# 32 bytes of padding behind each row of two TensorE operand buffers

## The chip, the cores and the metric

The kernel runs on one core of one Trainium2 chip. A core has five engines with their own instruction streams: TensorE (PE in the profile, with its weight loads as PEld), VectorE (DVE), ScalarE (ACT), GpSimd (POOL) and SyncE (SP), which issues most DMA transfers. SBUF is the working memory of 128 partitions; PSUM, in eight banks, takes TensorE's results. The metric is the device time of one execution in microseconds (us), as the median of several runs; lower is better.

## What is computed

Two transformer-like blocks over 256 tokens of width 2048, all in 32-bit floats. Cut to what matters here, the work is a chain of matrix products with 256 tokens on one side:

```
proj = rmsnorm(x) @ w_in                      # 2048 -> 7168, first block
x = x + mix @ w_out                           # attention and a gated recurrence in mix
x = x + softmax(q k) v @ w_mo                 # attention over 256 memory rows
x = x + (silu(a) * b) @ w_down                # a, b = conv(rmsnorm(x) @ w_up); 5632 wide
# second block: w_in_2, three conv mixers, w_out_2, then
f = (silu(gate) * val) @ w_down_2             # gate, val = conv(rmsnorm(x) @ w_up_2)
x = x + rms_norm(f)
```

## The kernel before

Each 32-bit matrix is split into a high part (rounded to the format fp32r, which TensorE multiplies in one pass) and a low part (the rest). A product A·B is then three products: hi·hi, lo·hi and hi·lo. The weights come in chunks of 128 partitions x 1024 floats: SP's queue loads a chunk to one of four slots of `raw`, ACT rounds it to `w_hi` (L784), DVE subtracts to make `w_lo` (L1325), and TensorE uses both. The semaphores `raw_loaded`, `hi_rounded`, `chunk_split` and `chunk_used` tie the four together, four chunks deep. Nothing of this is touched by the change.

The activations stand in two buffers with the same layout. `op` (the operand) has KT = 16 rows to a partition, one for each 128 features; `gu` (the gated buffer, named g in the profile) has FT = 44 rows. A row is 256 floats of the high part and behind them 256 floats of the low part, so it has 2048 bytes. `op_hi`, `op_lo`, `g_hi` and `g_lo` are views of them. `op` starts at byte 91456 of a partition and `gu` at the start of the arena, byte 124224; both are 320 past a multiple of 512 and so is each of their rows. `raw`, `w_hi` and `w_lo` start at 16512, 32896 and 49280, each 128 past such a multiple; a tile of 128 weights is 512 bytes, so each tile begins there too.

TensorE runs the products in three shapes, all through the helper `mm` (L2107):

- **The HHLL shape** (`product_halves` for up, down and up_2, and the parts of kind Q in `one_part`): the weight tile is stationary. Two matmuls of w_hi with the whole row (hi and lo, 512 columns), then two of w_lo with the row's first half (256 columns). A group is four matmuls, 1536 columns.
- **The three-times-256 shape** (parts of kind F, and conf, pool and gated in `product`): w_hi·hi, w_hi·lo, w_lo·hi for one weight tile, each with 256 columns; three matmuls, 768 columns.
- **The token-major shape** (hg_i, da_v, mem_v, out_2, down_2): 128 tokens of a row are stationary and 512 weights move past; three matmuls, 1536 columns. out_2 reads `y_hi` and `y_lo`, which the change doesn't pad.

```
mm(ps[:, 4 * parity + t], w_hi[:, s, cs], both[:, k].rearrange("p a t -> p (a t)"), k == 0, False)
mm(ps[:, 4 * parity + t, TOK:2 * TOK], w_lo[:, s, cs], both[:, k, 0], False, k == g.kt - 1)
```

In a line of the profile such as `ps<-op,w_hi`, the result is ps and the two operands follow; where the weights are stationary the activation stands first (`op,w_hi`), in the token-major shape it stands last (`w_hi,op`).

ACT writes the high parts (`round_pair`, `head_hi` and others), two or four rows with one instruction at most; DVE writes the low parts (`low_pair` L1398, `rest_of` L1390, `low` in `feed_forward`). Behind `gu` in the arena stand `up_s`, `cg` and `cv`, which hold the products of up while the convolution is made. The scratch for sums of squares, `sumsq` among it, is placed from the arena's end, at arena + 96928 + 4096 = byte 225248.

Of the kernel before, what the change touches and what calls it, by code (L numbers as in the profile page):

```python
# [19 lines left out]
F32R = mybir.dt.float32r  # L20
# [5 lines left out]
P = 128  # L26
TOK = 256
DM = 2048
KT = DM // P
FF = 5632  # L30
FT = FF // P
# [5 lines left out]
CONF_TAPS = 31  # L37
WB = 768
SLOTS = 4
CW = 1024  # L40
BANK = 512
EPS = 1e-6
# [6 lines left out]
UPAD = 2  # L49
# [38 lines left out]
def pieces_of(name, b):  # L88

    return [Piece(part.kind, part.bank + i, part.chunk + part.chunks) for part in parts_of(name, b) for i in range(part.tiles // 2)]  # L90
# [133 lines left out]
def build(nc, A):  # L224
# [4 lines left out]
    with ctx:  # L229
        at = [16512]  # L230

        def place(name, shape, dt=F32, offset=None):
            size = 4
            for d in shape[1:]:
                size *= d
            where = at[0] if offset is None else offset
            if offset is None:
                at[0] += (size + 31) // 32 * 32
            return nc.alloc_sbuf_tensor_at(name, shape, dt, offset=where)

        def sem(name):
            return ctx.enter_context(nc.semaphore(name))


        raw = place("raw", [P, SLOTS, CW])
        w_hi = place("w_hi", [P, SLOTS, CW], F32R)
        w_lo = place("w_lo", [P, SLOTS, CW], F32R)
        x_at = at[0]
# [10 lines left out]
        rstd = place("rstd", [P, 2, TOK])  # L259
        ones_r = place("ones_r", [P, P], F32R)  # L260
        op_at = at[0]
        op = place("op", [P, KT, 2, TOK], F32R)
        op_hi, op_lo = op[:, :, 0], op[:, :, 1]
        arena = at[0]
        end = 229344
        room = end - arena
        KB = 1024

        def inside(name, shape, offset, dt=F32):
            size = 4  # L270
            for d in shape[1:]:
                size *= d
            assert offset + size <= room, (name, offset, size, room)
            return place(name, shape, dt, offset=arena + offset)


        st = (room - 8 * KB) // 32 * 32
        sqb = inside("sqb", [P, 2, 2, TOK], st)
        sumsq = inside("sumsq", [P, 2, TOK], st + 4 * KB)
        sumsq_w = inside("sumsq_w", [P, 2, TOK], st + 6 * KB)  # L280
        sq_all = inside("sq_all", [P, 8, 2, TOK], 62 * KB)
        sq_in = inside("sq_in", [P, 8, 2, TOK], 0)
        hbuf = inside("hbuf", [P, 4, 2, TOK], 84 * KB)


        slab = lambda name, kb: inside(name, [P, HEADS, TOK], kb * KB)
        da_q, da_k = slab("da_q", 0), slab("da_k", 24)
        v_da, v_hg = inside("v_da", [P, 2, CW], 56 * KB), inside("v_hg", [P, 2, CW], 56 * KB)
        bias = slab("bias", 80)
# [28 lines left out]
        mp = inside("mp", [P, 2, TOK], 56 * KB)  # L318
        mp_t = inside("mp_t", [P, 2, 2, TOK], 58 * KB)

        gu = inside("g", [P, FT, 2, TOK], 0, F32R)
        g_hi, g_lo = gu[:, :, 0], gu[:, :, 1]
        up = inside("up_s", [P, 4, UPAD + TOK], 2 * FT * KB)
        cg = inside("cg", [P, 4, TOK], 2 * FT * KB + 16 * (UPAD + TOK))
        cv = inside("cv", [P, 4, TOK], 2 * FT * KB + 16 * (UPAD + TOK) + 4 * KB)

        y_hi = inside("y_hi", [P, KT, TOK], 0, F32R)
        y_lo = inside("y_lo", [P, KT, TOK], 16 * KB, F32R)
# [27 lines left out]

        raw_loaded = [sem(f"raw_loaded{i}") for i in range(SLOTS)]
        params_loaded, consts_loaded, norm_loaded = sem("params_loaded"), sem("consts_loaded"), sem("norm_loaded")
# [72 lines left out]
        def own_pieces(g, b, k):  # L431

            early = lambda p: p.kind == "F" and p.chunks < g.chunks
            return [i for i, p in enumerate(pieces_of(g.name, b)) if p.chunks + SLOTS - early(p) == k and p.chunks < g.chunks]

        def late_pieces(g, b, k, slots):

            if (g.name, b) in PARTS:
                return [i for i, p in enumerate(pieces_of(g.name, b)) if k == SLOTS and p.chunks == g.chunks]
            return [k - SLOTS] if slots is None else slots.get(k, ())  # L440
# [151 lines left out]
        def _(sp):  # L592
# [12 lines left out]
            sp.dma_start(raw[:, 0, 0:BANK], A["weights"][first_source, :, 0:BANK]).then_inc(first_loaded, 16)  # L605
            sp.dma_start(raw[:, 0, BANK:CW], A["weights"][first_source, :, BANK:CW]).then_inc(raw_loaded[0], 16)
            for c in range(1, KT):
# [167 lines left out]
        def _(act):  # L775
            steps = Steps(act, act_steps)

            def split(u, s):

                act.wait_ge(raw_loaded[s], 16 * u + 16)  # L780
                if not isinstance(u, int) or u > 0:

                    act.wait_ge(chunk_used, SLOTS * u + (s - SLOTS + 1))
                nc.scalar.activation(w_hi[:, s], raw[:, s], ACT.Copy).then_inc(hi_rounded, 1)  # L784
# [88 lines left out]
            act.wait_ge(raw_loaded[0], 16)  # L873
            nc.scalar.activation(w_hi[:, 0, BANK:CW], raw[:, 0, BANK:CW], ACT.Copy).then_inc(hi_rounded, 1)
            split(0, 1)
# [1920 lines left out]
```

## Time and profile before

| what | us |
|---|---|
| median of 3 runs | 2634.1 |
| lowest and highest | 2633.75 and 2635.73 |
| the profiled execution, its own time | 2635.15 |
| its span, first to last instruction | 2633.4 |
| PE busy in it | 2621.2 |
| PEld (weight loads, beside PE) | 2316.8 |
| DVE busy | 1789.2 |
| ACT busy | 1345.3 |
| POOL busy | 150.8 |
| mean granted TensorE clock | 0.999 of 2.4 GHz |

A matmul's duration in the profile runs past the start of the next one, since they are pipelined. What a matmul costs in a stream is the distance from its start to the start of the next, and the timeline gives the starts; its rows merge neighbours of the same kind, with their number behind x.

### The profile page before, as it was taken

Reading aid. Unit: us, or ns where it says so; the run is one execution under the profiler, and the core shown is the slowest. Engines: PE = TensorE matmul, PEld = TensorE weight load, DVE = VectorE, ACT = ScalarE, POOL = GpSimd, SP = SyncE. Lnnn points to the kernel's source line nnn. Section 1 sums busy time; section 2 is a strip of 40 time slices with the busy share of each in tenths; the row PEclk is TensorE's granted clock in tenths of the full one; section 3 lists DMA queues with packets and bytes.
Section 4 is the critical chain, followed back from the end, with each engine's and each line's share of the span. In section 5 each row is a group of like instructions: output and inputs, shape, how many; then the busy total and the mean of one; then the engine's idle time right before and its main releaser. Section 6 shows DMA issues by size and latency. Waiting matters only on the chain.

```text
span 2633.4 us, 41690 instructions
## 1 busy us (share of the span) xinstructions
PE 2621.2 (100%) x15689; PEld 2316.8 (88%) x15689; DVE 1789.2 (68%) x2188; ACT 1345.3 (51%) x1647; POOL 150.8 (6%) x106
## 2 busy tenths in 40 slices
PE   9999999999999999999999999999999999999999
PEld 9888898889999888888888889998888888888887
DVE  7677567566645777777775456998777777776444
ACT  6554375464533655555553344444665555554443
POOL 2001200000200200000001222000020000000000
PEclk9999999999999999999999999999999999999999
DMA  8555455546535555555555555655565555556554
GB/s 264 193 160 186 140 184 186 176 156 203 184 130 169 188 193 188 189 190 188 188 191 191 189 189 180 200 198 166 173 193 190 189 188 189 191 191 207 192 191 146
DMA packets 256256, 487.12 MB, mean 185 GB/s; under 512 B 15069, under 2 KB 80629, under 8 KB 255616
## 3 DMA queue, kind: packets, MB, share of 16 engines
q1 hardware_dynamic: 254496, 476.11, 54.7%
q0 software_dynamic: 1488, 9.19, 1.0%
q8 instruction: 92, 1.51, 0.2%
q14 instruction: 36, 0.29, 0.0%
q10 hardware_dynamic: 144, 0.01, 0.0%
HBM read 483.12 MB, written 2.13 MB: 184 GB/s over the span
## 4 chain that ended last, share of the span: by engine, by line
PE 92%; DVE 5%; ACT 1%; POOL 1%; issue 1%; DMA 0%; SPq 0%; DVEq 0%; ACTq 0%; POOLq 0%
PE ps L2107 92%; DVE w_lo L1325 2%; DVE acc L1854 2%; POOL sumsq L724 1%; DMA raw<-in_weights 0%; ACT w_hi L784 0%; DVE ua L1359 0%; DVE ya L1918 0%; DVE x_res L2088 0%; ACT lnz L1219 0%; PE ps L2640 0%; PE ps L2427 0%; DVE y_lo L1390 0%; DVE ya L1920 0%; DVE pa L1883 0%
## 5 line engine op out<-in xcount | busy, mean ns | idle before, releaser
L1325 DVE TENSOR_TENSOR w_lo<-raw,w_hi 128x1024 fp32r<-128x1024 f32 x899 | 1117.6, 1246 | 767.4 <-ACT w_hi L784 766.1
L2107 PE MATMUL ps<-op,w_hi 128*128 128x512 f32 (+1 forms) x6208 | 1615.0, 350 | 0.7 <-DVE op L1398 0.6
L784 ACT ACTIVATE w_hi<-raw 128x1024 fp32r<-128x1024 f32 x899 | 949.0, 1059 | 1083.3 <-PE ps L2107 1051.0
L2107 PEld LDWEIGHTS ps<-op,w_lo 128*128 128x128 f32 x5024 | 944.5, 188 | 163.8
L2107 PE MATMUL ps<-op,w_lo 128*128 128x256 f32 x5024 | 1086.7, 278 | 0.0
L2107 PEld LDWEIGHTS ps<-op,w_hi 128*128 128x128 f32 x6208 | 939.0, 188 | 5.2 <-issue 2.8
L2107 PE MATMUL ps<-g,w_hi 128*128 128x512 f32 x704 | 219.6, 393 | 0.0
L2107 PE MATMUL ps<-w_hi,g 128*128 128x512 f32 x704 | 218.3, 391 | 0.0
L2107 PE MATMUL ps<-w_hi,op 128*128 128x512 f32 x512 | 164.5, 396 | 0.0
L2107 PEld LDWEIGHTS ps<-g,w_lo 128*128 128x128 f32 x704 | 132.4, 188 | 30.0
L2107 PEld LDWEIGHTS ps<-w_hi,g 128*128 128x128 f32 x704 | 132.3, 188 | 27.9
L2107 PE MATMUL ps<-g,w_lo 128*128 128x256 f32 x704 | 138.8, 278 | 0.0
L2107 PE MATMUL ps<-w_lo,g 128*128 128x512 f32 x352 | 138.0, 392 | 0.0
L2107 PEld LDWEIGHTS ps<-w_hi,op 128*128 128x128 f32 x512 | 96.2, 188 | 22.2 <-issue 1.3
L2107 PEld LDWEIGHTS ps<-g,w_hi 128*128 128x128 f32 x704 | 106.0, 188 | 0.0
L2107 PE MATMUL ps<-w_lo,op 128*128 128x512 f32 x256 | 100.1, 391 | 0.0
L2107 PEld LDWEIGHTS ps<-w_lo,g 128*128 128x128 f32 x352 | 66.1, 188 | 15.4
L1854 DVE SCALAR_TENSOR_TENSOR acc<-glu,par,acc 128x256 f32<-128x256 f32 x180 | 74.9, 474 | 0.0
L1751 DVE SCALAR_TENSOR_TENSOR cg<-up_s,par,cg 128x256 f32<-128x256 f32 x176 | 73.3, 478 | 0.0
L1751 DVE SCALAR_TENSOR_TENSOR cv<-up_s,par,cv 128x256 f32<-128x256 f32 x176 | 73.3, 478 | 0.0
L2107 PEld LDWEIGHTS ps<-w_lo,op 128*128 128x128 f32 x256 | 48.1, 188 | 9.8
L1740 DVE TENSOR_TENSOR up_s<-up_s,rstd 128x1024 f32<-128x1024 f32 x44 | 53.9, 1225 | 1.5
(318 smaller groups left out, 1535.0 us busy)
## 6 DMA issues: line engine op xcount, KB each, us to landing
raw<-in_weights SPq DMA_DIRECT2D x899, 512.0 KB, 4.3
x_res<-in_x SPq DMA_DIRECT2D x8, 256.0 KB, 6.1
mem_x<-in_mem POOLq DMA_DIRECT2D x1, 2048.0 KB, 8.4
x_res<-in_x POOLq DMA_DIRECT2D x1, 2048.0 KB, 9.7
w_row<-row_dram POOLq DMA_DIRECT2D x2, 1024.0 KB, 7.4
out_x<-x_res SPq DMA_DIRECT2D x3, 512.0 KB, 2.9
rel_rev<-rel_dram POOLq DMA_DIRECT2D x1, 1024.0 KB, 7.7
hg_con<-in_hg_consts POOLq DMA_DIRECT2D x1, 576.0 KB, 5.3
```

What stands on the lines that cost most here:

```text
L724: steps.inc(TT(sumsq[:, :, :], squares[:, 0] if j == 1 else sumsq[:, :, :], squares[:, j], ALU.add))
L784: nc.scalar.activation(w_hi[:, s], raw[:, s], ACT.Copy).then_inc(hi_rounded, 1)
L1325: TT(w_lo[:, s], raw[:, s], w_hi[:, s].bitcast(F32), ALU.subtract).then_inc(chunk_split, 1)
L1740: TT(up[:, :, UPAD:UPAD + TOK], up[:, :, UPAD:UPAD + TOK], spread(rstd[:, 1], 4), ALU.mult).then_inc(up_scaled, 1)
L1751: ins = STT(buf[:, t], up[:, t, tap:tap + TOK], col(tap, kind, t, b), buf[:, t], ALU.mult, ALU.add)
L1854: ins = STT(acc[:, i], glu[:, i, tap:tap + TOK], pc("conv_b_w_2", 6 * tap + i), acc[:, i], ALU.mult, ALU.add)
L2107: return nc.tensor.matmul(out, lhsT, rhs, start=start, stop=stop, skip_group_check=True)
```

## The change

A constant ROW_PAD = 8 floats (32 bytes) is added behind each row of `op` and `gu`. The row pitch goes from 2048 to 2080 bytes. The sixteen rows of `op` then begin at sixteen different places within 512 bytes, 320 + 32·k modulo 512, and the 44 rows of `gu` go through these places 2.75 times. The views leave the padding out, so each row is still read and written as 512 neighbouring floats. `op` is 512 bytes longer, so the arena begins 512 bytes later; `gu` is 44·32 = 1408 bytes longer, and `up_s`, `cg` and `cv` move behind it. Everything counted from the arena's end stays at its byte. On every engine the instructions, their order and their semaphore waits are the same before and after.

```
@@ -37,6 +37,7 @@
 SLOTS = 4
+ROW_PAD = 8
 CW = 1024
@@ -259,12 +260,13 @@
         op_at = at[0]
-        op = place("op", [P, KT, 2, TOK], F32R)
+        op = place("op", [P, KT, 2 * TOK + ROW_PAD], F32R)[:, :, 0:2 * TOK].rearrange("p k (a t) -> p k a t", a=2)
         op_hi, op_lo = op[:, :, 0], op[:, :, 1]
         arena = at[0]
         end = 229344
         room = end - arena
         KB = 1024
+        GATED_END = FT * (2 * KB + 4 * ROW_PAD)
@@ -318,11 +320,11 @@
-        gu = inside("g", [P, FT, 2, TOK], 0, F32R)
+        gu = inside("g", [P, FT, 2 * TOK + ROW_PAD], 0, F32R)[:, :, 0:2 * TOK].rearrange("p k (a t) -> p k a t", a=2)
         g_hi, g_lo = gu[:, :, 0], gu[:, :, 1]
-        up = inside("up_s", [P, 4, UPAD + TOK], 2 * FT * KB)
-        cg = inside("cg", [P, 4, TOK], 2 * FT * KB + 16 * (UPAD + TOK))
-        cv = inside("cv", [P, 4, TOK], 2 * FT * KB + 16 * (UPAD + TOK) + 4 * KB)
+        up = inside("up_s", [P, 4, UPAD + TOK], GATED_END)
+        cg = inside("cg", [P, 4, TOK], GATED_END + 16 * (UPAD + TOK))
+        cv = inside("cv", [P, 4, TOK], GATED_END + 16 * (UPAD + TOK) + 4 * KB)
```

## Rows read from the trace of the kernel before

**Rows 1.** The page: busy time, share of the span and instructions; the chain by engine.

```profile
PE 2621.2 (100%) x15689; PEld 2316.8 (88%) x15689; DVE 1789.2 (68%) x2188; ACT 1345.3 (51%) x1647; POOL 150.8 (6%) x106
...
PE 92%; DVE 5%; ACT 1%; POOL 1%; issue 1%; DMA 0%; SPq 0%; DVEq 0%; ACTq 0%; POOLq 0%
```

**Rows 2.** Waits of TensorE, the longest: total us, times, longest.

```profile
PE ps L2107 <- DVE w_lo L1325: 1.7, 2, 1.5
```

**Rows 3.** TensorE's instructions by shape: count, busy us, mean ns, idle before.

```profile
L2107 PE MATMUL ps<-op,w_hi 128*128 128x512 f32 x3840 | 1201.1, 394 | 0.1
L2107 PE MATMUL ps<-op,w_lo 128*128 128x256 f32 x5024 | 1086.7, 278 | 0.0
L2107 PE MATMUL ps<-op,w_hi 128*128 128x256 f32 x2368 | 414.1, 280 | 0.6 <-DVE op L1398 0.6
L2107 PE MATMUL ps<-g,w_hi 128*128 128x512 f32 x704 | 219.6, 393 | 0.0
L2107 PE MATMUL ps<-w_hi,g 128*128 128x512 f32 x704 | 218.3, 391 | 0.0
L2107 PE MATMUL ps<-w_hi,op 128*128 128x512 f32 x512 | 164.5, 396 | 0.0
...
L2107 PE MATMUL ps<-w_hi,y_hi 128*128 128x512 f32 x128 | 51.3, 401 | 1.7 <-DVE w_lo L1325 1.7
```

**Rows 4.** Timeline of TensorE, three-times-256, at 670 us: start, length.

```profile
669.79 0.39 PE L2107 MATMUL ps<-op,w_hi 128*128 128x256 f32 x2
...
670.81 0.39 PE L2107 MATMUL ps<-op,w_hi 128*128 128x256 f32 x2
```

**Rows 5.** The same shape at 1750 us, in gated.

```profile
1749.73 0.40 PE L2107 MATMUL ps<-op,w_hi 128*128 128x256 f32 x2
...
1750.79 0.40 PE L2107 MATMUL ps<-op,w_hi 128*128 128x256 f32 x2
```

**Rows 6.** Timeline of TensorE, HHLL from op, in up at 1000 us.

```profile
999.71 0.62 PE L2107 MATMUL ps<-op,w_hi 128*128 128x512 f32 x2
1000.17 0.40 PE L2107 MATMUL ps<-op,w_lo 128*128 128x256 f32 x2
...
1001.79 0.62 PE L2107 MATMUL ps<-op,w_hi 128*128 128x512 f32 x2
```

**Rows 7.** TensorE in a stretch of down, HHLL from g: busy (matmuls), clock, DMA.

```profile
1400.00:1550.00 150.00, 150.00 (x867) 1.00 0.57 189
```

**Rows 8.** Timeline of TensorE, token-major from g, in down_2.

```profile
2500.06 0.62 PE L2107 MATMUL ps<-w_hi,g 128*128 128x512 f32 x2
...
2502.12 0.39 PE L2107 MATMUL ps<-w_hi,g 128*128 128x512 f32 x1
```

**Rows 9.** Timeline of TensorE, token-major from y, in out_2.

```profile
1795.02 0.40 PE L2107 MATMUL ps<-w_hi,y_lo 128*128 128x512 f32 x1
...
1796.42 0.40 PE L2107 MATMUL ps<-w_hi,y_lo 128*128 128x512 f32 x1
```

**Rows 10.** Timeline of TensorE, head means, ones_r stationary, eight matmuls of 512.

```profile
337.96 0.40 PE L2107 MATMUL ps<-hg_sq_high,ones_r 128*128 128x512 f32 x1
...
338.43 0.39 PE L2107 MATMUL ps<-hg_sq_high,ones_r 128*128 128x512 f32 x1
...
339.12 0.39 PE L2107 MATMUL ps<-hg_sq_low,ones_r 128*128 128x512 f32 x1
...
339.57 0.39 PE L2107 MATMUL ps<-hg_sq_low,ones_r 128*128 128x512 f32 x1
```

**Rows 11.** A stretch of up, PE, PEld, DVE, ACT, POOL busy (instructions), clock, DMA.

```profile
1000.00:1200.00 200.00, 200.00 (x1156) 175.44 (x1155) 145.76 (x171) 109.83 (x127) 0.00 (x0) 1.00 0.57 189
```

**Rows 12.** Matmuls that read sumsq, and that read lnz: ns min/median/max.

```profile
L2107 PE MATMUL ps<-sumsq,con x16: 378/379/454, 50.5 to 1925.8; 128*128 128x256 f32 x16
...
L2107 PE MATMUL ps<-lnz,con x12: 377/379/379, 1829.3 to 1831.7; 128*128 128x256 f32 x12
```

**Rows 13.** Timeline in up: DVE's split of one chunk and its idle time before.

```profile
1299.89 1.22 DVE L1325 TENSOR_TENSOR w_lo<-raw,w_hi 128x1024 fp32r<-128x1024 f32 x1 [0.85 <-ACT w_hi L784]
```

## The prediction

> **What bounds the kernel now.** I read the page first. Its busy line gives TensorE 2621.2 us of a span of 2633.4, and the chain that ended last is 92% TensorE [rows 1]. The view of waits then asks whether TensorE starves: its longest entry is 1.7 us in all [rows 2]. So the time is the sum of the distances between matmul starts, and the other engines matter only where they would make TensorE wait. The groups by shape give the counts, the timeline gives the distances, and I read one for each shape.
>
> - HHLL from `op`: groups start at 999.71 and, three later, at 1001.79, so 2.08/3 = 0.693 us for 1536 columns [rows 6]. From `gu` it is the same: 867 matmuls in 150 us, 4 × 150/867 = 0.692 [rows 7]. In up, 1156 matmuls in 200 us give 0.692 as well [rows 11].
> - Three-times-256: nine matmuls from 669.79 to 670.81 are 0.1133 us each [rows 4]; at 1750 us, same code and same places in SBUF modulo 512, nine take 1.06 us, 0.1178 each [rows 5]. About half of this shape runs at each pace.
> - Token-major from `gu`: nine matmuls from 2500.06 to 2502.12, 0.229 each, 0.687 for three [rows 8]. From `y`: six in 1.40 us, 0.233 each, 0.700 for three [rows 9].
>
> At 2.4 GHz (the stretches show a granted clock of 1.00 [rows 7, 11]) 1536 columns are 0.640 us, so each shape loses 6 to 10% of its time to something between the columns. If the change acts, it acts there.
>
> **The change, part by part.** It removes and adds no instruction; every engine keeps its order and waits. Four things move.
>
> *Places of the rows that TensorE reads.* Counts [rows 3]: 3840/2 + 704/2 = 1920 + 352 = 2272 HHLL groups; 2368/2 = 1184 groups of three times 256, 3552 matmuls; token-major 704/2 = 352 groups from `gu`, 512/2 = 256 from `op` (and 128 from `y`, whose row pitch stays). At today's paces these are 2272 × 0.692 = 1572 us, 3552 × 0.1156 (the mean of the two) = 411, 352 × 0.687 + 256 × 0.687 = 418, and 128 × 0.700 = 90: 2491 of the 2633.4. What would another place do? No operand row stands anywhere else modulo 512 than 320, so the trace can't price it directly; it can show how much the distances differ by themselves, and whether they follow place.
>
> They don't follow it much where I can look. (a) Two paces, 0.1133 and 0.1178, with the same places, in long unbroken stretches [rows 4, 5]: the pace is kept from whatever state the stream was in when it last restarted. (b) In nearly all products the activation row and the weight tile that is loaded meanwhile begin 192 bytes apart modulo 512 (320 against 128). In the head means both `ones_r` and the squares begin at 320, zero apart. There two matmuls take 0.47 us at first (337.96 to 338.43) and two take 0.45 near the end (339.12 to 339.57), 1.61/7 = 0.230 on the mean [rows 10]; the band with another distance is that of the token-major stretches, 0.229 and 0.233 [rows 8, 9]. (c) DVE busy for 145.76 of 200 us, ACT for 109.83 and DMA at 0.57 don't disturb the paces [rows 11]: HHLL is 0.69 per group wherever I look, so it isn't a meeting with other engines that the padding would space out. I take 0 for this edit.
>
> *Bounds of it, from both sides.* The fastest that the rows show is 0.225 for 512 columns (0.45/2 [rows 10]) and 0.1133 for 256 [rows 4]; the slowest 0.235 (0.47/2 [rows 10]) and 0.1178 [rows 5]. If each shape ran at its fastest: HHLL 2 × 0.225 + 2 × 0.1133 = 0.677, less 0.015 × 2272 = 34 us; three-times-256 less 0.0023 × 3552 = 8; token-major 0.675, less 0.012 × 608 = 7. Together −49 us. At the slowest: HHLL 2 × 0.235 + 2 × 0.1178 = 0.706, plus 0.014 × 2272 = 32; three-times-256 plus 0.0022 × 3552 = 8; token-major 3 × 0.235 = 0.705, plus 0.018 × 608 = 11. Together +51 us.
>
> By the Trainium skill (TensorE: Matmul & The Clock Gate, Back-to-back issue gap) an isolated matmul costs N/2.4 + 2.5 ns, some 216 ns for 512 columns and 109 for 256. The rows here show 0.225 to 0.235 and 0.113 to 0.118, so the trace is slower than that rule in each shape; if the places were the whole of the difference and the change took it away, an estimate by that page would be 2 × 0.216 + 2 × 0.109 = 0.650 for HHLL, which is 0.042 × 2272 = 95 us less in that shape alone.
>
> *Places of the rows that ACT and DVE write.* A pair of rows or four rows now step by 520 floats and not by 512. These writes are off the path: in up DVE has 0.85 us of idle time before the 1.22 us split of a chunk [rows 13], and TensorE's waits on it sum to 1.7 us in the whole kernel [rows 2]. Any slowing up to that idle time is hidden; if the cover were gone, w_lo would be late next and TensorE would wait at `chunk_split`. Cost 0; on both sides I allow a microsecond.
>
> *`up_s`, `cg`, `cv` and the arena.* They are read and written by DVE and ACT alone, under the same cover. The arena moves by 512 bytes, so nothing else in it changes place modulo 512. Cost 0, and again a microsecond at most.
>
> *The state after a restart.* Even if places don't count in themselves, the stream may fall into the other pace after one of its interruptions, in some stretches of three-times-256 (±8 us if all went one way, as above) and in out_2 (128 groups at 0.687 and not 0.700: −2). The single runs lie within 2 us of each other, so the same program mostly takes the same paces; another program need not. This gives ±4 us about zero.
>
> Sum: 0. The profiled execution is 2635.15 by its own time, 2633.4 in span, so 1.75 lies around it; it is 1.05 above the median of the runs. With a sum of zero I forecast the median, 2634.
>
> **The rivals.**
>
> *Faster, −5 to −49 us: the two reads of TensorE meet.* A weight load begins with a matmul and reads 512 bytes while the row is read beside it. With every pair at the same 192 bytes from each other the meeting is the same each time, and spreading rows would avoid it for most. For it: the 6 to 10% lost in every shape, and its regularity. Against it: the head means with zero distance lose as much [rows 10], and one set of places has two paces [rows 4, 5]. Midway, −27 us: 2607. Chance 0.26.
>
> *Slower, +5 to +51 us: odd rows start half-way into a unit of reading.* All rows now start at a multiple of 64 bytes; padded by 32, every odd row is off by 32. If TensorE fetched the moving row in units of 64 bytes (16 columns), each matmul on an odd row would fetch one unit more, 0.1133/16 = 0.007 us. The matmuls with an activation row moving are 3840 + 5024 + 2368 + 704, and 704 of w_lo with `gu`, one for each 512 wide one, 12,640; half of them, 6320 × 0.007 = 44 us: 2678. It decides from 5.3/6320 = 0.8 ns a matmul on. Against it: `sumsq` starts at 225248, which is 32 past a multiple of 64, `lnz` at 203072 is not, and both read 256 columns in a median of 379 ns [rows 12]. But those are plain f32 matmuls, slower by nature, which may hide it. It could also be that a change of place at each new row keeps throwing the stream into its slow pace, with the bound of +51. Midway, +27 us: 2661. Chance 0.27.
>
> By the Trainium skill (SBUF — State Buffer, Specifications (TRN2)) SBUF has 16-byte cachelines. A padding of 32 bytes keeps each row at the start of one, so by that page the odd rows cost nothing more, and the estimate is no change; no run here shows the size of such a line.
>
> *The change doesn't do what it says:* the weight side keeps its one place, and a weight load of 512 bytes passes over all of a period of 512 bytes whatever the row's start, so a meeting happens once whichever place the row has. That ends at my forecast, 2634, and is part of its chance.
>
> **How the numbers follow.** No change gets 0.47: within 0.2% of 2634.1, or ±5.3 us, which is about what a measurement of this kernel can tell from no change. Its own range is 2629 to 2639. Faster 0.26, slower 0.27, spread over their stretches with more weight near the small end. Leaving out about 0.1 at each far end gives 2604 at the low side (−30) and 2662 at the high side (+28). The chances of the three signs are those of the three cases.
>
> **What would show it.** In the changed kernel's profile: HHLL at 0.692 in up, in down and in up_2 (1156 matmuls in 200 us), token-major at 0.687 in down_2, the two paces of three-times-256, 0.1133 and 0.1178, perhaps in other stretches, and TensorE's wait for w_lo still a microsecond or two. The faster rival would show more than 1156 matmuls in 200 us of up; the slower one fewer, and within up a difference between rows of even and odd number, which is its own mark: eight matmuls on one row and eight on the next. The prediction is wrong if the place of a row within 512 bytes enters the distance between matmuls at all; since nearly every matmul has such a row, 1 ns each already makes 13 us.

## The result and the profile after

The changed kernel takes 2668.44 us (median of 4 runs, 2668.02 to 2668.74) against 2634.36 for the kernel before: a ratio of 1.0129, 95% interval 1.0111 to 1.0146. It is 34 us slower. The forecast was no change, and the time lies above its range of 2604 to 2662.

The page of the changed kernel first: the busy line, then the chain by engine. They answer to [rows 1]. The number of matmuls is the same, and TensorE's busy time has grown by 34.5 us, which is the whole loss. DVE, ACT and POOL take what they took.

```profile
PE 2655.7 (100%) x15689; PEld 2338.3 (88%) x15689; DVE 1790.2 (67%) x2188; ACT 1345.2 (50%) x1647; POOL 150.2 (6%) x106
...
PE 95%; DVE 4%; ACT 1%; DMA 0%; issue 0%; SPq 0%; DVEq 0%; ACTq 0%
```

The view of waits of TensorE, against [rows 2]: the wait for w_lo is even shorter. So TensorE starves no more than before.

```profile
PE ps L2109 <- DVE w_lo L1327: 1.2, 2, 1.0
```

TensorE's instructions by shape, against [rows 3]: all that read a padded buffer have a longer mean duration, by 2 to 4 ns; the last row, out_2 with its unpadded `y`, has not.

```profile
L2109 PE MATMUL ps<-op,w_hi 128*128 128x512 f32 x3840 | 1208.6, 396 | 0.1
L2109 PE MATMUL ps<-op,w_lo 128*128 128x256 f32 x5024 | 1098.6, 281 | 0.0
L2109 PE MATMUL ps<-op,w_hi 128*128 128x256 f32 x2368 | 424.6, 283 | 0.6 <-DVE op L1400 0.6
L2109 PE MATMUL ps<-g,w_hi 128*128 128x512 f32 x704 | 221.3, 396 | 0.0
...
L2109 PE MATMUL ps<-w_hi,y_hi 128*128 128x512 f32 x128 | 51.0, 398 | 1.2 <-DVE w_lo L1327 1.2
```

The count of matmuls in a fixed stretch is the quickest gauge (TensorE alone: busy, matmuls, clock, DMA share, GB/s; a count takes in one or two matmuls that only reach into the stretch). The rows are up, up_2 and down_2. Before, up had 1156 [rows 11]; 1142 means 1.2% longer distances, at the same granted clock of 1.00 and with the DMA engines as busy as before (0.59 against 0.57).

```profile
1000.00:1200.00 200.00, 200.00 (x1142) 1.00 0.59 187
...
2100.00:2300.00 200.00, 200.00 (x1140) 1.00 0.59 187
2420.00:2540.00 120.00, 120.00 (x519) 1.00 0.60 189
```

The timeline of the changed kernel in up shows it in the distances: four HHLL groups from 999.75 to 1002.56 are 2.81/4 = 0.703 us each, against 0.693 [rows 6].

```profile
999.75 0.63 PE L2109 MATMUL ps<-op,w_hi 128*128 128x512 f32 x2
...
1002.56 0.63 PE L2109 MATMUL ps<-op,w_hi 128*128 128x512 f32 x2
```

From here on I also use the mean distance over the starts of all matmuls of a shape in a trace. The few beside a restart (an interruption of the stream by a wait or by other matmuls) are left out. Such a mean is good to about a tenth of a nanosecond. By them HHLL in up went from 693.3 to 701.7 ns (up_2 702.9, down 703.0), three-times-256 from 115.3 to 118.2 a matmul, token-major from `gu` from 228.9 to 232.1 and from `op` from 229.2 to 232.1; from `y` it stayed (229.9 and 229.1). Both traces have the same 15,689 matmuls in the same order, so the distances can be subtracted one by one. HHLL takes 19.1 us more, three-times-256 10.5 and token-major 5.6 (3.4 from `gu`, 2.2 from `op`); what reads `y` takes 0.3 less and the restarts 1.6 less. Together that is the 33.2 us by which the span grew.

Two more things stand in those starts. Within up, the 16 rows k of `op` differ from each other, and the second eight repeat the first, to 0.1 ns; rows of even and odd number have the same mean, 701.6 and 701.7. Here is the mean HHLL group by row over 20 blocks:

```
row k       0      1      2      3      4      5      6      7      8      9     10     11     12     13     14     15
ns      699.9  700.5  699.2  700.7  704.7  701.6  702.5  704.1  700.0  700.4  699.2  700.8  704.6  701.6  702.5  704.1
```

Before the change all sixteen lie between 693.3 and 693.4. And at a fixed position of the block each distance comes back, from block to block, with a standard deviation of 0.6 ns. So this isn't noise. The repeat after eight rows points to the addresses, since eight rows shift the place by 256 bytes.

### The profile page after: what moved, and what is told of

The parts are those of the page before. It is cut to its first block, busy times and chain, and to the rows that moved or that the text cites. A ratio compares the mean times of both kernels' runs of the same rounds, so it can differ in the third digit from the quotient of the medians.

```text
span 2666.6 us, 41690 instructions
## 1 busy us (share of the span) xinstructions
PE 2655.7 (100%) x15689; PEld 2338.3 (88%) x15689; DVE 1790.2 (67%) x2188; ACT 1345.2 (50%) x1647; POOL 150.2 (6%) x106
## 4 chain that ended last, share of the span: by engine, by line
PE 95%; DVE 4%; ACT 1%; DMA 0%; issue 0%; SPq 0%; DVEq 0%; ACTq 0%
PE ps L2109 94%; DVE w_lo L1327 1%; DVE acc L1856 1%; DMA raw<-in_weights 0%; ACT w_hi L786 0%; DVE ya L1920 0%; DVE x_res L2090 0%; DVE ua L1361 0%; ACT lnz L1221 0%; PE ps L2642 0%; PE ps L2429 0%; DVE y_lo L1392 0%; DVE ya L1922 0%; DVE cvp L1910 0%; DVE ya L1916 0%
## 5 line engine op out<-in xcount | busy, mean ns | idle before, releaser
L2109 PE MATMUL ps<-op,w_hi 128*128 128x512 f32 (+1 forms) x6208 | 1633.0, 353 | 0.7 <-DVE op L1400 0.6
L2109 PE MATMUL ps<-op,w_lo 128*128 128x256 f32 x5024 | 1098.6, 281 | 0.0
L2109 PEld LDWEIGHTS ps<-op,w_hi 128*128 128x128 f32 x6208 | 953.8, 189 | 5.4 <-issue 2.8
```

The costliest lines, as they stand in the source:

```text
L2109: return nc.tensor.matmul(out, lhsT, rhs, start=start, stop=stop, skip_group_check=True)
```

## The experiments

After the result I held three theories. **O**, the slower rival on record: a row off a multiple of 64 bytes costs one unit more. **S**: the steps from one place to the next cost; one place for all rows, whichever it is, lets the stream settle. **P**: each place, relative to the weights, has its own price in each shape. A place is named by how far it lies from that of before: +64 is 64 bytes further.

### The two buffers apart

In `op_pad32` only `op` is padded, in `gu_pad32` only `gu`:

```
-        op = place("op", [P, KT, 2, TOK], F32R)
+        op = place("op", [P, KT, 2 * TOK + 8], F32R)[:, :, 0:2 * TOK].rearrange("p k (a t) -> p k a t", a=2)
...
-        gu = inside("g", [P, FT, 2, TOK], 0, F32R)
+        gu = inside("g", [P, FT, 2 * TOK + ROW_PAD], 0, F32R)[:, :, 0:2 * TOK].rearrange("p k (a t) -> p k a t", a=2)
```

> Half of the change: 32 bytes behind each row of op alone, gu with its 2048 bytes. The HHLL groups from op are 1920 of 2272, all 1184 groups of three times 256 and 256 of the 608 token-major ones read op. All theories that place the cost in TensorE's reading of the rows give down at 0.693 again, up at 0.702, and a total of some 28 of the 34 us: 2662. A cost that lies in the moved arena or in gu's writes would leave more with gu: under 2655 here.

> The other half: gu alone padded, op and the start of the arena as before. 352 HHLL groups at 0.703 and not 0.693 (+3.5 us) and 1056 token-major matmuls at 0.232 and not 0.229 (+3.4): 2641, with up at 0.693. A cost in the moved up_s, cg and cv would show in up as well and give more.

Measured: 2661.59 (ratio 1.0104, 1.0087 to 1.0121) and 2641.25 (1.0027, 1.0015 to 1.0038), so +27.4 and +7.1, together the +34 of the change. The windows of up, down, up_2 and down_2 with `op` alone padded: up and up_2 are slow, down and down_2 are as before.

```profile
1000.00:1200.00 200.00, 200.00 (x1142) 1.00 0.59 187
1400.00:1550.00 150.00, 150.00 (x868) 1.00 0.59 190
2100.00:2300.00 200.00, 200.00 (x1140) 1.00 0.58 186
2420.00:2540.00 120.00, 120.00 (x526) 1.00 0.61 193
```

And with `gu` alone padded: down and down_2 are slow, up is as before although `up_s`, `cg` and `cv` stand elsewhere. The cost goes with the reading of the padded rows by TensorE, and with nothing else that moved.

```profile
1000.00:1200.00 200.00, 200.00 (x1156) 1.00 0.59 189
1400.00:1550.00 150.00, 150.00 (x856) 1.00 0.58 186
...
2420.00:2540.00 120.00, 120.00 (x518) 1.00 0.60 189
```

### One place for all rows, eight of them

The pitch stays 2048 bytes; a gap ahead of `op` moves `op`, `gu`, `y` and the rest of the arena together, by 32 up to 256 bytes (`off32` to `off256`). The gap of `off32` is 8 floats; that of `off256` is 64:

```
+        gap = place("gap", [P, 8])
         op = place("op", [P, KT, 2, TOK], F32R)
```

> The row pitch stays 2048 bytes as before; 32 bytes are left free ahead of op, so that op, gu and the whole arena begin 32 bytes later. All rows have one place modulo 512 again, 352 and no longer 320. Theory S (the steps cost: with one place for all rows the stream settles in a short repeating pattern, with a new place at each row it never does): as before, 2634 within 3 us, HHLL groups at 0.693 us. Theory P (each place has its own price, and the place of before happens to be a cheap one): another time, anywhere between 2600 and 2700, HHLL groups not at 0.693. Theory O (the slower rival on record: a row off a multiple of 64 bytes costs one unit of 0.007 us more): twice the 44 us of the forecast, since all rows are now off, so 2722.

> As off32 with 64 bytes: all rows at 384 modulo 512, which is the same place modulo 256 as the weight tiles (128). S: 2634 within 3 us. P: another time than before and than off32; if the meeting of the two reads is worst where they begin together, above 2668. O: 2634, since rows are on multiples of 64.

> 96 bytes further than before: rows at 416 modulo 512, 32 past the weight tiles' place modulo 256. P: a time of its own, by its neighbours some 2650 to 2675. If places off a multiple of 64 are the dear ones (702.7 ns a group at +32 against 693.3 and 696.7 at 0 and +64), this one has some 0.703 as well.

> Constant place again, 128 bytes further than before: rows at 448 modulo 512. If the period of the effect is 256 bytes, as the repetition of the changed kernel's rows by eight says, this is a place of its own, 64 bytes past the weight tiles' modulo 256. Theory P (each place relative to the weights has its own steady pattern and price): a time of its own between 2615 and 2680, one steady repeating pattern without any dependence on the row. Theory S (only steps cost) is already in trouble: it would give 2634.

> 192 bytes further: rows at 0 modulo 512, 128 past the weight tiles' place modulo 256. P: a time of its own between 2615 and 2680, with one pattern for all rows. S: 2634. If what counts is how far the two starts are from each other in either direction, this is the farthest point and should be the best.

> Constant place, 160 bytes further than before (96 past the weight tiles' place modulo 256). The constant places so far gave 0.6933 us for an HHLL group at +0, 0.7027 at +32, 0.6967 at +64, 0.6933 at +96, 0.6900 at +128 and 0.6967 at +192, a mean of 0.6955, and the changed kernel, which goes through all eight, has 0.7017. Theory P alone (each row pays the price of its place) needs 0.7017 x 8 = 5.614 in all, so 0.720 on the mean for +160 and +224, and a total of some 2690 for this kernel. Theory P with steps (a place has a steady price, and each step from one place to the next costs on top until the stream has settled) lets both lie within the band of the others, 0.690 to 0.703, total 2635 to 2675.

> Constant place, 224 bytes further (160 past the weight tiles' place modulo 256). As for the kernel at +160: P alone 0.720 and 2690, P with steps within 0.690 to 0.703 and 2635 to 2675.

> Constant place, 256 bytes further. If the effect repeats with 256 bytes, the steady patterns are those of before to the nanosecond: HHLL 0.6933, token-major 0.2289, and a total within 5 us of 2634, the rest being which of its two paces three-times-256 falls into after a restart. If the period is 512, HHLL has another value.

Measured, with the mean distances in ns (HHLL in up, per group; the others per matmul, token-major from `gu`):

| moved by | median us | ratio, 95% interval | HHLL | three-times-256 | token-major |
|---|---|---|---|---|---|
| 0 (before) | 2634 | 1 | 693.3 | 115.3 | 228.9 |
| 32 | 2672.98 | 1.0147, 1.0130 to 1.0164 | 702.7 | 118.3 | 233.3 |
| 64 | 2652.41 | 1.0070, 1.0053 to 1.0087 | 696.7 | 119.9 | 226.7 |
| 96 | 2649.83 | 1.0058, 1.0042 to 1.0075 | 693.3 | 116.9 | 233.3 |
| 128 | 2643.38 | 1.0035, 1.0022 to 1.0047 | 690.0 | 117.5 | 233.3 |
| 160 | 2683.20 | 1.0185, 1.0168 to 1.0202 | 706.7 | 120.0 | 234.3 |
| 192 | 2660.49 | 1.0100, 1.0083 to 1.0117 | 696.7 | 119.0 | 232.4 |
| 224 | 2674.01 | 1.0151, 1.0134 to 1.0168 | 703.3 | 118.0 | 233.3 |
| 256 | 2633.72 | 1.0000, 0.9991 to 1.0010 | 693.3 | 114.8 | 228.9 |

S falls: with a constant place the time isn't that of before. O falls as well: at +32 every row is off a multiple of 64 and the loss is 39 us where O wanted 88, +96 costs 16, and +192, on a multiple of 64, costs 27. P stands as a statement on constant places: each has its own distances in each shape, the order of the places is different in each shape, and at +256 HHLL and token-major come back exactly. The window of up at +128 (cheapest for HHLL) and at +160 (dearest), one kernel after the other:

```profile
1000.00:1200.00 200.00, 200.00 (x1162) 1.00 0.59 190
```

```profile
1000.00:1200.00 200.00, 200.00 (x1134) 1.00 0.58 185
```

At +64 down_2, token-major, has more matmuls in its window than the 526 of before, while three-times-256 is nearly the slowest; the window of down_2, then the timeline of conf, where nine matmuls from 1649.79 to 1650.87 take 1.08 us, 0.120 each.

```profile
2420.00:2540.00 120.00, 120.00 (x531) 1.00 0.60 194
```

```profile
1649.79 0.40 PE L2108 MATMUL ps<-op,w_hi 128*128 128x256 f32 x2
...
1650.87 0.40 PE L2108 MATMUL ps<-op,w_hi 128*128 128x256 f32 x2
```

Three-times-256 needs more care, since its mean can mix two paces. At the place of before it runs at 113.3 or 117.8 ns from one restart to the next [rows 4, 5], and at +128 it has the same two paces. Here are nine matmuls of `off128` from 371.16 to 372.18, 0.1133 each, and nine from 1649.99 to 1651.05, 0.1178 each:

```profile
371.16 0.28 PE L2108 MATMUL ps<-op,w_lo 128*128 128x256 f32 x1
...
372.18 0.28 PE L2108 MATMUL ps<-op,w_lo 128*128 128x256 f32 x1
...
1649.99 0.28 PE L2108 MATMUL ps<-op,w_lo 128*128 128x256 f32 x1
...
1651.05 0.28 PE L2108 MATMUL ps<-op,w_lo 128*128 128x256 f32 x1
```

At the place of before (or +256) the fast pace holds for 47 to 70% of this shape, over six programs (before, `gu_pad32`, `off256`, `all32`, `up128`, `by_product`); at +128 it holds for 7%. No other constant place shows the pace of 113.3 at all. So the 7.7 us that three-times-256 costs at +128, nearly all of that kernel's +9, may be as much a matter of which pace it fell into as of the place. One program can't tell.

Do TensorE's reads meet the work of VectorE and ScalarE, which write the weight slots, and not each other? The traces show no such effect. Of the HHLL groups from `op` before, from 870 to 2400 us, 850 ran beside DVE work for over 90% of their length and 162 beside none; both have a mean of 693.3. For ACT work it is 693.3 (408 groups) and 693.4 (370). At +160, in down, 131 groups beside DVE work and 64 beside none both have 706.7. DMA ran throughout and can't be set apart like this, but all the groups from `op` in that stretch before deviate from each other by 0.5 ns only.

At +256 the windows of up, down, up_2 and down_2 are those of before:

```profile
1000.00:1200.00 200.00, 200.00 (x1155) 1.00 0.59 189
1400.00:1550.00 150.00, 150.00 (x867) 1.00 0.59 190
2100.00:2300.00 200.00, 200.00 (x1156) 1.00 0.59 189
2420.00:2540.00 120.00, 120.00 (x526) 1.00 0.60 191
```

### The weights moved along

`all32` puts the gap of 32 bytes ahead of `raw`, so that weights and operands move together:

```
+        gap = place("gap", [P, 8])
         raw = place("raw", [P, SLOTS, CW])
```

> 32 bytes are left free ahead of raw, so that the weights and the operands all begin 32 bytes later: absolute places change, the distance between them doesn't. P with the relative place (the two reads of TensorE meet): 2634 within 3 us and HHLL at 0.693. A cost of starting off a multiple of 64 bytes in itself: 2660 or more, as the kernel that moves the operands alone by 32 bytes.

Measured: 2638.25 (1.0015, 1.0006 to 1.0025), with HHLL at 693.3, token-major at 228.9 from `gu` and 229.2 from `op`, as before. The windows of up, down, up_2 and down_2:

```profile
1000.00:1200.00 200.00, 200.00 (x1157) 1.00 0.61 189
1400.00:1550.00 150.00, 150.00 (x867) 1.00 0.61 190
2100.00:2300.00 200.00, 200.00 (x1156) 1.00 0.60 189
2420.00:2540.00 120.00, 120.00 (x526) 1.00 0.61 192
```

So for this shift what counts is the distance between the two operands, not where either stands. The total is 4.5 us above the kernel before of the same comparison, and not within 3. In the profiled execution, the slowest of its ten, three-times-256 spent more time in its slower pace (115.7 and not 115.3, 1.6 us), and 3.9 us lie beside restarts, most of it in out_2; TensorE's wait for w_lo is 3.7 us and not 1.7. Which pace three-times-256 takes isn't set by the distance: 1640 to 1680 us had 355 matmuls before and 1740 to 1780 us 342, and here it is the other way round.

```profile
PE ps L2108 <- DVE w_lo L1326: 3.7, 3, 2.9
...
1640.00:1680.00 40.00, 40.00 (x342) 1.00 0.57 185
1740.00:1780.00 40.00, 40.00 (x356) 1.00 0.61 207
```

### Two places in turn

`op_pad128` has 128 bytes behind each row of `op`, so that rows alternate between two places whose prices are both known:

```
+        op = place("op", [P, KT, 2 * TOK + 32], F32R)[:, :, 0:2 * TOK].rearrange("p k (a t) -> p k a t", a=2)
```

> 128 bytes behind each row of op, gu as before: rows of op alternate between two places modulo 256, those of before (HHLL 0.6933, three-times-256 0.1153, token-major 0.2292) and of +128 (0.6900, 0.1175, 0.2332). P alone: HHLL 0.6917 in up, three-times-256 0.1164, so -0.0016 x 1920 + 0.0011 x 3552 + 0.0020 x 768 = +2 us, 2636. P with steps: up above both of its places, over 0.6933, and the total over 2640.

Measured: 2657.10 (1.0087, 1.0070 to 1.0104). HHLL in up is 705.0, dearer than either of its places (693.3 and 690.0); in up_2, where the order within a chunk takes the two rows in turn, it is 696.7, also above both. Three-times-256 is 116.2, between its two, token-major from `op` 231.9, also between (229.2 and 233.2). The windows of up and up_2:

```profile
1000.00:1200.00 200.00, 200.00 (x1136) 1.00 0.58 187
...
2100.00:2300.00 200.00, 200.00 (x1150) 1.00 0.59 188
```

So in HHLL the price of a changing place isn't the mean of the places. Changing places cost something on top, as S says, in that one shape; whether each step costs by itself, or the changing place only leads into a dearer pattern, is open, since fewer steps (up, one in eight matmuls) cost more here than many (up_2, one in each). In the changed kernel too: HHLL's eight places have a mean of 697.8, it has 701.7 to 703.0. In the other two shapes the mean of the eight places is what it has: 118.1 against 118.2, and 231.9 against 232.1.

Only the means agree. A single row of the changed kernel doesn't pay the price of its own place. In the table of rows above, row 4 stands at +128, the cheapest place for HHLL, and is the dearest with 704.7; row 5 stands at +160, the dearest, and has 701.6. In down_2 the rows lie between 231.8 and 232.5, where constant places go from 226.7 to 234.3.

### The cheapest place for each product

Two kernels use the table. `up128` lets up and up_2 alone read their operand at +128; it is written 128 bytes ahead of the others' place, which is the same modulo 256. `by_product` adds `gu` at +128 for down, at +64 for down_2, and `y` at +64 for out_2:

```
+        gap = place("gap", [P, 64])
         op_at = at[0]
         op = place("op", [P, KT, 2, TOK], F32R)
+        op_up = place("op_up", [P, KT, 2, TOK], F32R, offset=op_at - 128)
...
+        gu = inside("g", [P, FT, 2, TOK], 128, F32R)
+        gu_2 = inside("g_2", [P, FT, 2, TOK], 64, F32R)
...
+        y_hi = inside("y_hi", [P, KT, TOK], 64, F32R)
+        y_lo = inside("y_lo", [P, KT, TOK], 16 * KB + 64, F32R)
```

> The operand of up and up_2 alone begins 128 bytes ahead of the other operands' place, which modulo 256 is the place of +128, the cheapest for HHLL among the eight constant ones (0.6900 us a group); every other product reads op where it did modulo 256. Places alone set the price within a product: HHLL in up and up_2 0.6900 and in down 0.6933, so 1408 groups x 0.0033 = 4.7 us less, 2629, within the 4 us that the paces of three-times-256 move. If the cheap reading at +128 was a chance of that program and not of the place, up stays at 0.6933 and the time at 2634.

> The kernel with the operand of up and up_2 at +128, and besides gu at +128 for down (HHLL 0.6900), gu at +64 for down_2 and y at +64 for out_2 (token-major 0.2267 and not 0.2289 and 0.2299). If the prices by place hold product by product: 4.7 + 352 x 0.0033 = 1.2, + 1056 x 0.0022 = 2.3, + 384 x 0.0026 = 1.0, so 9.2 us less, 2625, again within some 4 us for three-times-256. If the paces depend on more than the place, less than half of it.

Measured: 2630.62 (0.9985, 0.9976 to 0.9994) and 2627.91 (0.9978, 0.9968 to 0.9987). The distances are those of the table in each product: HHLL in up 690.0 in both, token-major from `gu` 226.7 and from `y` 227.1 in `by_product`. The windows of up, down, up_2 and down_2 of `by_product`:

```profile
1000.00:1200.00 200.00, 200.00 (x1161) 1.00 0.60 190
1400.00:1550.00 150.00, 150.00 (x872) 1.00 0.61 191
2100.00:2300.00 200.00, 200.00 (x1162) 1.00 0.59 189
2420.00:2540.00 120.00, 120.00 (x531) 1.00 0.61 193
```

The total fell by 6.6 us and not by 9.2. Matmul by matmul, against the trace of the kernel before, the chosen places gave what was forecast: 5.8 us in HHLL, 2.3 in down_2 and 1.1 in out_2. Three-times-256 took 0.9 back (115.6 a matmul and not 115.3) and the restarts 0.5; that makes 7.8 between the two traces, where the medians are 6.6 apart. In HHLL and token-major a price therefore belongs to the constant place of a product and not to the program, and this version is faster than both kernels.

## Why the prediction was wrong, point by point

**What bounds the kernel, the counts, the paces and the terms at nothing** were right. TensorE's distances are the whole of the time; the writes of ACT and DVE, the arena and `up_s`, `cg` and `cv` cost nothing that shows, since padding either buffer slows only the products that read it. Two readings were a little off without effect: the 0.700 us for `y` came from one stretch (the mean is 3 × 229.9 ns = 0.690), and the middle of +5 and +51 is 28, not 27.

**The step that failed is the 0 for "places of the rows that TensorE reads".** It rested on two readings. Reading (b) took the head means, with a distance of zero, to lie in the same band as the products with a distance of 192, and concluded that the distance doesn't matter [rows 10]. But the band was 225 to 235 ns, 4% wide, and a difference of 0.2% was to be excluded. At +64 the distance is zero modulo 256, and there the runs show HHLL +3.4 ns, three-times-256 +4.6 ns, token-major −2.2, in all +18 us. Eight matmuls that were still changing from 0.47 to 0.45 for two could not show it. Reading (a) was true and not to the point: a shape can have two paces at one place [rows 4, 5], and the place still decides which paces there are. The pace of 113.3 ns held for 58% of three-times-256 before and for 4% after, and that loss is most of this shape's 10.5 us. That the trace had no row at another distance was said there; it should have moved the chance from "no change" to the two sides.

**The bounds held in the sum, and not in each term.** They were −49 and +51 us, from the fastest and the slowest distance of each shape. The dearest constant place took +49, the changed kernel +34. But three-times-256 was given 0.1178 us at worst, and it took 0.1182 in the changed kernel and 0.120 at +64 and +160; HHLL at +160 (0.7067) is just past its 0.706. Of the eight constant places none is faster as a whole than that of before, so the mean over all of them lies above it. No row of its trace told that, and the range should have gone up to the bound.

**The slower rival** had the sign and nearly the size (+44 against +34), but its mechanism is not what happened. Its own mark, a difference between even and odd rows, is absent (701.6 and 701.7 in up), and moving weights and operands together by 32 bytes costs 4.5 us where moving the operands alone costs 39. The last mechanism named beside it, that a change of place at each row keeps the stream in its slow pace, came nearer: three-times-256 lost its fast pace, and HHLL costs more with changing places than at their mean. It holds only in part, since constant places cost as well. **The faster rival** named the right two operands, the row and the weight tile, and had the sign wrong: the distance of 192 bytes was a good one. That their reads meet in time is not shown; the runs show only that the distance counts. **"The change doesn't do what it says"** leaned on a weight load passing all places whatever the row's start; off32 to off224 refute that.

**The size.** Of the 34 us the means over the eight places give 4.5 × 2272 = 10 in HHLL, 2.8 × 3552 = 10 in three-times-256 and 3.0 × 1824 = 5 in token-major. The other 9 of HHLL's 19.1 us come on top with the change of place itself; no sum of places gives their size, and what makes them is open.

The sentence on SBUF's lines led the same way as the wrong step. The Trainium skill (SBUF — State Buffer, Specifications (TRN2)) gives cachelines of 16 bytes. All rows here, at every place, began at multiples of 16, and the kernels still differed by up to 1.9% of the whole time, so that line size didn't decide the cost.

## What to carry to other kernels

Where TensorE is the bound, try the start of the activation rows relative to the start of the weight tiles, modulo 256 bytes. In this kernel the cheapest and the dearest constant place lie 1.9% apart, and choosing a place for each product gained 0.2% on the kernel before; how much another kernel has to gain was not run. One gap ahead of a buffer tests a place, and the count of matmuls in a fixed window reads it in each product. Try constant places first and choose by product. Rows spread over several places took the mean of them or more here. A narrow band of distances in a trace is evidence for "no change" only when it is narrower than the change that is to be excluded.

## What the runs showed of the hardware that was not expected

The mean HHLL group at the constant places is 690.0, 693.3, 696.7, 700.0, 703.3 or 706.7 ns, and 702.7 once: all but that one are steps of 3.33 ns from each other, eight columns at 2.4 GHz. Behind each stands a short repeating pattern of distances (before: 226, 236, 118, 113 ns).

One place can hold more than one pattern. At +160 up_2 runs at 700.0 ns and up at 706.7. The order of the weight tiles isn't the reason by itself, for down has up_2's order and also runs at 706.7. The windows of down and up_2 at +160:

```profile
1400.00:1550.00 150.00, 150.00 (x851) 1.00 0.59 186
2100.00:2300.00 200.00, 200.00 (x1145) 1.00 0.59 188
```

Why +160 (96 bytes past the weight tiles' place modulo 256) is the dearest for HHLL, and why the place of before, +64 and +128 are each cheap in one shape and not in another, is open. The runs give the prices, not the circuit behind them.
